# Width-2 window sums as a difference of neighbours, later summed-square matmuls, and a planner that knows a wait between dependent VectorE operations

## What is computed

```python
def rmsnorm(x, g):
    xf = x.astype(jnp.float32)
    y = xf * lax.rsqrt(jnp.mean(xf * xf, axis=-1, keepdims=True) + RMS_EPS)
    return (y * g.astype(jnp.float32)).astype(x.dtype)

def pool_mixer(u, hist, offset, w_grp, scale):
    # u (B,T,E), hist (B,POOL_HIST,E); trailing-window means via cumulative sums.
    B, T, E = u.shape
    h = jnp.concatenate([hist.astype(u.dtype), u], axis=1).astype(jnp.float32)   # (B, 15+T, E)
    cs = jnp.concatenate([jnp.zeros_like(h[:, :1]), jnp.cumsum(h, axis=1)], axis=1)  # cs[k] = sum h[:k]
    pos = offset + jnp.arange(T)
    means = []
    for g, w in enumerate(POOL_WINDOWS):
        c0, c1 = g * POOL_GROUP, (g + 1) * POOL_GROUP
        s = cs[:, POOL_HIST + 1:, c0:c1] - cs[:, POOL_HIST + 1 - w:POOL_HIST + 1 - w + T, c0:c1]
        cnt = jnp.minimum(pos + 1, w).astype(jnp.float32)[None, :, None]   # no padding counted
        means.append(s / cnt)
    d = (jnp.concatenate(means, axis=-1) - u.astype(jnp.float32)).astype(u.dtype)
    d = d.reshape(B, T, N_POOL_GROUPS, POOL_GROUP)
    y = jnp.einsum('btgc,gcd->btgd', d, w_grp).reshape(B, T, E) * scale
    return y, h[:, -POOL_HIST:].astype(u.dtype)
```

## Time and profile before

| | us |
|---|---|
| median of the runs | 3667.92 |
| lowest run | 3662.28 |
| the profiled execution | 3648.3 |
| its span on the slowest core (6) | 3646.7 |
| TensorE busy on it (matmuls) | 3431.3 |
| VectorE busy | 2531.0 |
| ScalarE busy | 1578.4 |
| GpSimd busy | 673.2 |

### The profile page before, as it was taken

The page is one execution under the profiler, slowest core; times in us unless marked ns, Lnnn a source line. Parts: engine busy times, 40 slices in busy tenths (PEclk is TensorE's granted clock), DMA queues, the critical chain, the costliest instruction groups (busy, mean ns, idle before and its releaser), DMA issues.

```text
span 3646.7 us, 57618 instructions; the slowest of 8 cores (3607.4 to 3646.7 us)
## 1 busy us (share of the span) xinstructions
PE 3431.3 (94%) x17839; PEld 1652.1 (45%) x18185; DVE 2531.0 (69%) x3786; ACT 1578.4 (43%) x2425; POOL 673.2 (18%) x1345
## 2 busy tenths in 40 slices
PE   7899899998999999798999999979999999999997
PEld 2344444444554454344444444445444444444444
DVE  6767787764877876876986455555545777777776
ACT  3333343335777785555554333323332233333332
POOL 2112221211343343011001011111001121111111
PEclk9999999999999999899999999989999999999998
DMA  7688766767665656999877454575434753333224
GB/s 137 154 221 174 206 138 161 189 182 235 150 147 135 148 142 210 275 278 275 271 256 235 137 176 157 162 236 170 156 116 159 234 175 114 116 110 105 90 94 163
DMA packets 254347, 637.38 MB, mean 175 GB/s; under 512 B 45320, under 2 KB 58888, under 8 KB 245216
## 3 DMA queue, kind: packets, MB, share of 16 engines
q0 software_dynamic: 74448, 300.45, 32.5%
q1 hardware_dynamic: 179600, 333.22, 28.7%
HBM read 553.78 MB, written 188.84 MB: 204 GB/s over the span
## 4 chain that ended last, share of the span: by engine, by line
PE 73%; DMA 11%; DVE 8%; issue 4%; ACT 2%; POOL 1%; SPq 1%; DVEq 0%; ACTq 0%; POOLq 0%; another core or an unknown queue 0%
PE ps L647 43%; PE ps L799 21%; PE ps L1497 6%; DMA arena<-xin 2%; DMA arena<-yd 2%; DMA arena<-wq 2%; DMA yd<-arena 2%; DMA arena<-wst 2%; DVE arena L739 1%; DVE arena L729 1%; POOL arena L1315 1%; PE ps L1236 1%; DVE arena L953 1%; PE ps L1581 1%; PE ps L861 1%
## 5 line engine op out<-in xcount | busy, mean ns | idle before, releaser
L647 PE MATMUL ps<-arena 128*128 128x512 bf16 (+1 forms) x10146 | 2140.8, 365 | 83.1 <-DMA arena<-wq 18.2
L647 PEld LDWEIGHTS ps<-arena 128*128 128x128 bf16 x10368 | 967.1, 99 | 1127.7 <-issue 105.9
L799 PE MATMUL ps<-arena 128*128 128x512 bf16 (+1 forms) x4517 | 961.7, 365 | 32.1 <-DVE arena L1408 7.7
L799 PEld LDWEIGHTS ps<-arena 128*128 128x128 bf16 x4608 | 432.9, 99 | 523.1 <-issue 50.0
L604 POOL DMA_DIRECT2D arena<-wq x437 | 231.1, 529 | 1408.1 <-PE ps L799 485.8
L696 ACT ACTIVATE arena<-arena 128x512 bf16<-128x512 f32 (+1 forms) x360 | 210.7, 590 | 626.0 <-DVE arena L803 554.1
L953 DVE TENSOR_TENSOR_SCAN arena<-arena 128x527 f32<-128x527 f32 (+1 forms) x288 | 342.1, 1188 | 89.0 <-ACT arena L938 84.8
L803 DVE TENSOR_TENSOR arena<-ps,arena 128x512 f32<-128x512 f32 (+1 forms) x288 | 185.1, 643 | 220.2 <-PE ps L799 205.5
L970 ACT ACTIVATE arena<-ps 128x512 f32<-128x512 f32 (+1 forms) x288 | 161.4, 560 | 235.8 <-PE ps L647 213.5
L938 ACT ACTIVATE arena<-ps 128x512 f32<-128x512 f32 x256 | 152.3, 595 | 224.2 <-PE ps L647 173.4
L979 DVE SCALAR_TENSOR_TENSOR arena<-arena 128x512 bf16<-128x512 f32 (+1 forms) x288 | 206.3, 717 | 51.1 <-DVE arena L960 30.8
(11 more groups left out here) (100 smaller groups left out, 2642.8 us busy)
## 6 DMA issues: line engine op xcount, KB each, us to landing
arena<-wq POOLq DMA_DIRECT2D x437, 512.0 KB, 5.6
xs<-arena SPq DMA_DIRECT2D x192, 256.0 KB, 6.3
arena<-xs SPq DMA_DIRECT2D x192, 256.0 KB, 6.4
wq<-wst POOLq DMA_DIRECT2D x72, 512.0 KB, 8.6
arena<-hd SPq DMA_DIRECT2D x34, 1024.0 KB, 7.5
arena<-xin SPq DMA_DIRECT2D x128, 256.0 KB, 10.4
arena<-wst POOLq DMA_DIRECT2D x64, 512.0 KB, 9.4
yd<-arena SPq DMA_DIRECT2D x128, 256.0 KB, 5.1
```

The source lines that it names most:

```text
L647: r = e.matmul(P[:, 0:T], lhsT=W[:, k * 256 + base:k * 256 + base + 128], rhs=H[:, k * st:k * st + T], start=(k == 0), stop=(k == 7))
L799: r = e.matmul(P[:, 0:T], lhsT=W[:, k * 128:(k + 1) * 128], rhs=ym[k].ap(BF16)[:, 0:T], start=(k == 0), stop=(k == 15))
```

## The change

Three edits. (1) In the pooling layers the width-2 tiles (channel tiles 0 to 3) of all groups but the first no longer use the scan and the combine: one subtraction gives u[t−1] − u[t], and the factor 1/2 goes into the scale column, in a small constant `ps2` that two GpSimd operations fill at the start. The other tiles keep the code, moved to `slide`. (2) `sq_stat` returns nothing for the six squares without a matmul; the two others of a `norm0` wait 6 and 8 ticks and its finish 10, where `one` is not set; `limit` is applied only where `one` is set. `outproj` keeps 7 ticks. (3) In the planner a VectorE operation that depends on the VectorE operation placed just before it is ready 0.17 us after that one's end, and a scan of n columns costs 2.39 n + 110 ns in place of 2.083 n + 80.

```diff
@@ Sched.schedule
+        drain = dict.fromkeys(ENGS)
...
+                    if drain[e] in o.deps and tf + 0.17 > rt:
+                        rt = tf + 0.17
...
             free[e] = st + cost
+            if e == "dve":
+                drain[e] = o
@@ c_scan
-    return (2.083 * n + 80) / 1000
+    return (2.39 * n + 110) / 1000
@@ Build.sq_stat
...
-                return lambda: None
+                return None
...
@@ Build.norm0
+        one = now or g == 8
         for k in range(8):
-            self.limit("sq", 3 if now else 5)
-            self.later(3, self.sq_stat(xt, k, T, st, now or g == 8 or False), "sq")
+            if one:
+                self.limit("sq", 3 if now else 5)
+            f = self.sq_stat(xt, k, T, st, one)
+            if f is not None:
+                self.later(3 if one else 5 + k // 2, f, "sq")
...
-            self.later(3, fin)
+            self.later(3 if one else 10, fin)
@@ Build.outproj
-            self.limit("sq", 3 if self.ph == "B" else 5)
-            self.later(7, self.sq_stat(xt, m, T, st, one), "sq")
+            if one:
+                self.limit("sq", 3 if self.ph == "B" else 5)
+            f = self.sq_stat(xt, m, T, st, one)
+            if f is not None:
+                self.later(7, f, "sq")
@@ Build.pool_cts
+            par = self.par
+            if w == 2 and g > 0:
+
+                par, sc = self.ps2, j * 4 + ct
+                S.add("dve", lambda e, u=u, src=src: e.tensor_tensor(out=V(src, 15, n), in0=V(u, 30, n), in1=V(u, 31, n), op=ALU.subtract),
+                      reads=[(u, 0), (u, 1)], writes=[src], cost=c_tt(T))
+            else:
+                sc = P_PSCALE + j * 16 + ct
+                self.slide(u, src, w, L, V, n, T, g, gq)
...
-                return e.scalar_tensor_tensor(out=a, in0=b, scalar=self.par[:, P_PSCALE + j * 16 + ct:P_PSCALE + j * 16 + ct + 1],
+                return e.scalar_tensor_tensor(out=a, in0=b, scalar=par[:, sc:sc + 1],
...
+    def slide(self, u, src, w, L, V, n, T, g, gq):
...
@@ Build.consts
+        self.ps2 = self.fix(8, F32)
...
+        for j in range(2):
+            ops.append(S.add("pool", lambda e, j=j: e.tensor_scalar(
+                out=self.ps2[:, 4 * j:4 * j + 4], in0=self.par[:, P_PSCALE + 16 * j:P_PSCALE + 16 * j + 4], scalar1=0.5, scalar2=None,
+                op0=ALU.mult), reads=["par"], cost=0.2))
```

More of the change, by code:

```diff
@@ L952, in pool_cts @@
             src = self.sab.tile()
[L953 to L961, removed]
-                reads=[src, (u, 1)], writes=[src], cost=c_stt(T, False))
+            par = self.par
[6 more added lines that the diff above has]
+                self.slide(u, src, w, L, V, n, T, g, gq)
             wz = self.chunk(("z", j, ct // 2))
@@ L973, in pool_cts, with yf @@
             ym.append(y)
-            def yf(e, src=src, z=z, y=y, ct=ct):
+            def yf(e, src=src, z=z, y=y, par=par, sc=sc):
                 a, b, c = y.ap(BF16)[:, 0:T], V(src, 15, n), z.ap()[:, 0:T]
@@ L978, in yf @@
                     a, c = a.rearrange("p (s t) -> p s t", s=4), c.rearrange("p (s t) -> p s t", s=4)
-                return e.scalar_tensor_tensor(out=a, in0=b, scalar=self.par[:, P_PSCALE + j * 16 + ct:P_PSCALE + j * 16 + ct + 1],
+                return e.scalar_tensor_tensor(out=a, in0=b, scalar=par[:, sc:sc + 1],
                                               in1=c, op0=ALU.mult, op1=ALU.mult)
             S.add("dve", yf, reads=[src, z], writes=[y], cost=c_stt(T))
+    def slide(self, u, src, w, L, V, n, T, g, gq):
+        S = self.S
+        S.add("dve", lambda e: e.tensor_tensor_scan(
+            out=src.ap()[:, 0:L - 16], data0=u.ap()[:, 16:L], data1=u.ap()[:, 16 - w:L - w], initial=0.0,
+            op0=ALU.add, op1=ALU.subtract), reads=[(u, 0), (u, 1)], writes=[src], cost=c_scan(L - 16))
+        if g == 0:
+            S.add("dve", lambda e: e.tensor_tensor(
+                out=src.ap()[:, 15:30], in0=src.ap()[:, 15:30], in1=self.bc[:, B_RATIO + gq * 16:B_RATIO + gq * 16 + 15], op=ALU.mult),
+                reads=[src, "bcr"], writes=[src], cost=0.1)
+        S.add("dve", lambda e: e.scalar_tensor_tensor(
+            out=V(src, 15, n), in0=V(src, 15, n), scalar=1.0 / w, in1=V(u, 31, n), op0=ALU.mult, op1=ALU.subtract),
+            reads=[src, (u, 1)], writes=[src], cost=c_stt(T, False))
     def ulast_rows(self, g, h):
```

## The result

The changed kernel takes 3632 us (median of its runs); beside runs of the kernel before on the same chip the ratio is 0.989, 95% interval 0.984 to 0.994. Run again later beside the experiments it was 0.9927 (0.9898 to 0.9956). So it is faster by some 27 to 40 us (1% is 36.5 us), which lies within the 2% called no change here. The forecast was 3647, 20.5 us won, with a range of 3618 to 3674. The size came out about right; the experiments show that the step which was to carry it carries nothing.

What follows compares the result with a forecast made beforehand. TensorE was taken to bound the kernel, idle about 215 us. Moved matmuls 19.5, planner 0 and width-2 sums 1 made 20.5 us, from 3667.9 to 3647; forecast's own range 3637 to 3660, whole range 3618 to 3674.

Steps and rivals of the forecast that it cites:

- What bounds the kernel: TensorE, busy 94% of the span; 82 us idle in the first pooling layer, nothing to win in the last.
- near 820: Sign of being right: the first pooling layer ends near 820 us.
- The matmuls moved later: First-layer norms: summed-square matmuls get more TensorE work ahead, covering 20.1 us of stalls; 19.5 us won after weight waits.
- The first rival: First-layer stalls only change name: planner's times set the order, or projections wait for weights; gain 0 to 6, chance 0.20.
- The weights that I feared behind the moved matmul: Projections pulled ahead wait for weight transfers on full DMA engines: 1.8 us at each of three long stalls, 5.4 us.
- the clock stay at 1.00: Sign of being right: granted clock stays 1.00 behind the first-layer stalls, where 5.4 us were lost to the lower clock.
- Width-2 sums: Both pooling layers: 75.8 us less VectorE work; 0 in the first layer's sample group, 1 us in the closing stretch.
- The planner's numbers: Truer VectorE times re-sort the whole list but only hide VectorE time beside a full TensorE: 0 on the path.
- The third rival: New order worth more: sample group's 6.8 and 3.6 us and half the convolution's wait go; 17 us more, 3630, chance 0.13.
- half of the convolution's 14.1 us: Part of the third rival: half of the convolution projections' 14.1 us wait for L1243 would go.
- the fourth rival: Re-sorting costs: independent 3.35 us reciprocals overtake scans; ten felt by TensorE lose 33 us beside 20.5 won, 3680; chance 0.05.
- the second rival: Output blocks of five groups: frame buffers come free too late, 33 us lost beside 20.5 won, 3680; chance 0.10.

Runs made afterwards that it cites:

- the two halves of the 0.17 us: Kernel before plus the 0.17 us either only as time added in the planner's model (0.9977) or only in choosing the next VectorE operation (0.9968).
- the scan's wrong price: Kernel before with the planner's scan cost lowered to 1.776 n + 50 ns, further from the trace: 1.0 (0.9974 to 1.0026).

## Why the prediction was right in size and wrong in its main step

**What bounds the kernel.** Right in the main. TensorE is full, the last pooling layer gave nothing (from the last start of the gated MLP's first matmuls, L1497, to the end of the span it is 814 us before and 813 after, in the mean of the cores), and the gain lies in the first layer, which ends at 782 and not 802; "near 820" had taken the window of 840 for the stage. Two readings were off. The 215 us of idle time contain matmuls whose records are missing; on the six cores with all records it is 178. And 0.218 us a matmul divides by the 3064 records, where the 3125 weight loads of the same row give 0.213; that moves no term by more than 0.3 us. What cost more is the window: by beginning at 200 us it left out TensorE's waits for VectorE's copies at the start, 8.1 us of which the third edit takes 6.1 away.

**The matmuls moved later: 19.5 us, measured 0** (1.0005, so −8 to +12 us). The step that failed is "so k=3 gets three more projections ahead of it, 5.2 us, and k=7 gets four projections and an output block". Ticks move an operation in the writing, and I let that stand for its place on the engine. At the three long stalls the order didn't change by one matmul. The first rival said just this, "the planner sets the order by its own times, the ticks only the priority", and had 0.20; it belonged ahead of the forecast, because `schedule` takes an operation by priority only among those that are ready. The weights that I feared behind the moved matmul (5.4 us) were never put to the test. Nor did the clock stay at 1.00 behind these places: after a stall of 3.6 us that ended at 545.27 in the changed kernel the granted clock is 0.50 from 545 to 549 us.

**Width-2 sums: 1 us, measured 15 alone** (0.9959) **and nothing beside the third edit** (0.9928 without them, 0.9927 with). The working of the prices held (681 ns for 688). The step that failed is the shares of busy time: "beside a VectorE that works 608 of 840 us" reads a mean as slack. TensorE's waits up to the end of the first layer fall by 6.4 us with this edit alone and the cost of the lower clock by 8.3. They come where VectorE is late for a short while, and there 5 us less a group would count; that the planner's order has taken these places already in the full change fits the times, but wasn't shown place by place.

**The planner's numbers: 0 on the path, measured 24 us** (0.9933; the 0.17 us alone 0.9927). I costed what the gap could hide, VectorE time beside a full TensorE, and left the new order to two rivals. The third rival, "the new order is worth more", named the right cause and the sample group's waits of 6.8 and 3.6 us, which are gone in the profile after; it had 0.13, as an extra to the forecast. Its other part, half of the convolution's 14.1 us, gave nothing: 573.2 us from the first to the last sigmoid before, 574.5 after, in the mean of the cores. The reciprocals of the fourth rival cost nothing that shows.

The Trainium skill's rule (VectorE: DVE Perf Modes, "The DRAIN you can't avoid") would have the third edit hide nothing. The trace disagrees: 78 waits of 0.17 us became 62 when independent operations could go between. The section itself sends the reader on to another, by which an operation that isn't held starts earlier; that fits the 0.67 against 0.92 us of the earlier trace rows. That VectorE time can be hidden was read rightly, and 38 us of it were; that it is worth 0 on the path was not.

**The sum.** Two wrong terms nearly made up for each other: 19.5 too much, 24 missing. That the size came out is luck, and the range held for that reason.

**Buffers and weights.** What the second rival feared does show: VectorE's add waits 20.1 us for frame loads in the first layer where it waited 2.5; with the second edit alone it is 10.2, with the third alone 10.3. But of the rival's 33 us only about 2 reach TensorE: what failed in it is the price. That the third edit alone has half of it too shows that the later norm matmuls aren't its only source.

**Open.** Why the two halves of the 0.17 us give 8 and 12 us but 27 together: their intervals (0.9956 to 0.9998 and 0.9936 to 1.0001) allow a plain sum of up to 39 us, and the ends of the first layer nearly add up (6.3 and 12.1 us earlier, 21.7 with the whole third edit), so there may be nothing to explain. No gap longer or shorter than 0.17 us was tried, so it isn't shown that this value is the best, nor that a truer plan rather than just this new order is what helps; that three kernels with the whole third edit in other company and one with the 0.17 us alone gain too, and the scan's wrong price doesn't, speaks for it. And the same idea with the model's DMA times, the other input on which the norm's place depends, wasn't tried.

## What to carry to other kernels

Where a planner writes the order, an edit to priorities or to the place of writing is worth nothing until the lists before and after have been compared at the stall; an edit to the modelled times is an edit to the order everywhere. Telling the planner of a gap of 0.17 us gave 27 us (0.9927); 72 us less work on the engine that has the gap gave 15 (0.9959). Read the waits of the whole stage, its start too, and on more than one core: 6.1 of the 14.6 us of waits won here lay outside the window that was read. And try each part of a bundle alone: here one part carried the whole, one was swallowed by it, and the one with the best story did nothing.

## What was not expected of the hardware

The neighbours 0 and 1, 2 and 3, 4 and 5, 6 and 7 differ: one core of each pair is faster over the span, by 22 to 32 us in the profile before and by 19 to 26 in that after, and it isn't the same one in both (0, 3, 5, 7 before; 1, 2, 5, 6 after). In the profiles of the experiments it is 15 to 39 us, once 1. Cores 4 to 7 of the changed kernel:

```profile
core 4: 3628.1 us, clock 0.980
core 5: 3601.8 us, clock 0.980
core 6: 3593.6 us, clock 0.982
core 7: 3612.4 us, clock 0.982
```

Much of it is there by the end of the first layer (before: 811.0 and 792.5 us on cores 4 and 5, 813.8 and 796.5 on 6 and 7). The time reported is that of the slower neighbours, so a wait read on the slowest core is one of a core that is late: the norm matmul's wait for VectorE after the change is 17.0 us on core 4 and 9.4 in the mean. What the two share that would do this was not tested.
